# First gate chunks of the sparse block moved ahead of the keys and values, and the first block's input squared by tokens

## What is computed

```python
# first block
x = x + 0.5 * swiglu_ffn(rmsnorm(x, ffn1_norm), w_gate, w_up, w_down)    # width 1024 -> 2816 -> 1024
x = x + hybrid_mixer(rmsnorm(x, mix_norm), ...)
x = x + 0.5 * swiglu_ffn(rmsnorm(x, ffn2_norm), ...)
x = rmsnorm(x, final_norm)
# second block: twice x = layer_norm(alpha * x + mixer(x)); the sparse mixer, 8 heads of 128:
q, ckv, kr, qi, ki, wi, gate = split(x @ w_in)       # queries; 128-wide latent; 32-wide rotary key; index parts; gate 1024
q = rope(q); ckv = rms_norm(ckv); kr = rope(kr); qi = rope(qi); ki = rope(ki)
isc = sum_h(relu(qi_h . ki) * wi_h)                  # causal; each token keeps its 64 best keys
k = concat(ckv @ w_uk, kr); v = ckv @ w_uv           # in effect
o = softmax(q k^T over the kept keys) v
y = (silu(gate) * o) @ w_out
```

## Time and profile before

| | |
|---|---|
| median of three runs | 749.05 us (747.11 to 749.78) |
| the profiled execution | 747.19 us |
| its span in the trace | 745.4 us |
| TensorE busy, mean granted clock | 722.1 us (97%), 0.987 of full |
| VectorE, ScalarE, GpSimd busy | 447.5, 351.7, 73.0 us |
| HBM read | 126.77 MB, 171 GB/s over the span |

### The profile page before, as it was taken

One profiled execution on the slowest core, in us unless ns is written; L12 is line 12 of the kernel. 1 busy time (PEld: TensorE's weight loads), 2 busy tenths in 40 slices (PEclk: granted clock), 3 DMA queues, 4 the chain that ended last, 5 costly groups with the idle time before them and its releaser, 6 DMA issues.

```text
span 745.4 us, 11354 instructions
## 1 busy us (share of the span) xinstructions
PE 722.1 (97%) x4596; PEld 650.0 (87%) x4596; DVE 447.5 (60%) x707; ACT 351.7 (47%) x457; POOL 73.0 (10%) x43
## 2 busy tenths in 40 slices
PE   7999999999999999999999999999999999987985
PEld 6999999988887889999999888889998988766874
DVE  5875656655476446656566655485543657893655
ACT  5643334535377546534434444466335444564351
POOL 4000000000001320000000000000017260420002
PEclk8999999999999999999999999999999999999997
DMA  8986455545355344645545574265545133631001
GB/s 246 351 351 262 169 176 190 198 170 197 142 189 207 113 174 153 240 173 187 203 169 172 180 270 173 110 229 195 197 170 193 58 113 113 226 113 56 1 1 57
DMA packets 20535, 128.37 MB, mean 172 GB/s; under 512 B 2416, under 2 KB 3312, under 8 KB 6160
## 3 DMA queue, kind: packets, MB, share of 16 engines
q1 hardware_dynamic: 20448, 127.70, 48.0%
q0 software_dynamic: 48, 0.13, 0.1%
HBM read 126.77 MB, written 1.05 MB: 171 GB/s over the span
## 4 chain that ended last, share of the span: by engine, by line
PE 93%; DVE 2%; ACT 2%; DMA 1%; POOL 1%; issue 1%; SPq 0%; DVEq 0%; POOLq 0%; ACTq 0%
PE ps L368 29%; PE ps L370 28%; PE ps L369 28%; PE ps L565 1%; DMA work<-in_xt 1%; PE ps L379 1%; PE ps L622 1%; PE ps L621 1%; PE ps L903 1%; PE ps L620 1%; DVE wlo L1364 1%; PE ps L736 1%; ACT whi L978 1%; PE ps L892 0%; PE ps L611 0%
## 5 line engine op out<-in xcount | busy, mean ns | idle before, releaser
L368 PE MATMUL ps<-xth,whi 128*128 128x256 f32 x832 | 237.3, 285 | 4.4 <-DVE wlo L1501 4.4
L369 PE MATMUL ps<-xtl,whi 128*128 128x256 f32 x832 | 236.6, 284 | 0.0
L370 PE MATMUL ps<-xth,wlo 128*128 128x256 f32 x832 | 236.6, 284 | 0.0
L978 ACT ACTIVATE whi<-raw 128x2048 fp32r<-128x2048 f32 x78 | 148.6, 1909 | 100.3 <-PE ps L370 97.6
L1364 DVE TENSOR_TENSOR wlo<-raw,whi 128x2048 fp32r<-128x2048 f32 x68 | 156.7, 2314 | 64.3 <-ACT whi L978 64.2
L368 PEld LDWEIGHTS ps<-xth,whi 128*128 128x128 f32 x832 | 161.0, 194 | 5.2 <-DVE xtl L1377 5.1
L369 PEld LDWEIGHTS ps<-xtl,whi 128*128 128x128 f32 x832 | 161.0, 194 | 0.1
L370 PEld LDWEIGHTS ps<-xth,wlo 128*128 128x128 f32 x832 | 160.9, 193 | 0.0
L368 PE MATMUL ps<-whi,xth 128*128 128x512 f32 (+1 forms) x304 | 122.8, 404 | 3.2 <-DVE xtl L1493 2.0
L370 PE MATMUL ps<-whi,xtl 128*128 128x512 f32 (+1 forms) x304 | 117.9, 388 | 0.0
L369 PE MATMUL ps<-wlo,xth 128*128 128x512 f32 (+1 forms) x304 | 117.5, 387 | 0.0
(11 more groups left out here) (209 smaller groups left out, 681.0 us busy)
## 6 DMA issues: line engine op xcount, KB each, us to landing
raw<-in_gu SPq DMA_DIRECT2D x41, 1024.0 KB, 4.8
raw<-in_dn SPq DMA_DIRECT2D x22, 1024.0 KB, 4.7
raw<-in_win SPq DMA_DIRECT2D x8, 1024.0 KB, 4.8
raw<-in_fqk SPq DMA_DIRECT2D x8, 1024.0 KB, 5.0
raw<-in_wout SPq DMA_DIRECT2D x4, 1024.0 KB, 4.9
raw<-in_fg SPq DMA_DIRECT2D x4, 1024.0 KB, 5.0
raw<-in_fv SPq DMA_DIRECT2D x4, 1024.0 KB, 4.7
raw<-in_fo SPq DMA_DIRECT2D x4, 1024.0 KB, 4.7
```

The costliest lines, as they stand in the source:

```text
L368: pe.matmul(o, xh, wh, start=start, stop=False)
L369: pe.matmul(o, xh, wl, start=False, stop=False)
L370: return pe.matmul(o, xl, wh, start=False, stop=stop)
L978: act.activation(whi[:, c % RING, 0:n], raw[:, c % RING, 0:n], ACT.Copy).then_inc(hi_ready, 1)
```

## The change

In the first block: `sm` and the first piece of chunk 1 are issued by ScalarE; `X` is loaded in two halves right behind chunk 3, ahead of chunk 4; GpSimd's squares go, and `norm(0)` squares X on ScalarE (two passes), with the reciprocal and two diagonals on VectorE; the row is formed by TensorE in the middle of chunk 3, copied by ScalarE between the conversions of chunks 4 and 5, and VectorE scales chunk 0 behind the splits of chunks 4 and 5. In the sparse block: both gate chunks go into banks 2 and 3 around `turn_queries(1)`, ahead of the keys; heads 4 to 7 of the keys wait for the Silus (`gate_ready`); scores 0 and 1 come ahead of the values, which use banks 2 and 3 twice; ScalarE applies Silu and loads the Exp table ahead of the key copies, and copies the values between the first exponentials; the copy of bank 3 stands ahead of exps(4); four chunk conversions and four splits of the output chunks have other places.

```diff
@@ SP: loads @@
-            sp.dma_start(sm[:, :], a["sm"]).then_inc(sm_landed, 16)
...
-                for c in range(2):
+                for c in range(2 if i else 1):
                     sp.dma_start(raw[:, c, cols], a["gu0"][c][:, cols])...
...
             chunk(3, a["gu0"][3])
+            for t in range(NT):
+                sp.dma_start(X[:, t, :], a["x"][:, t, :]).then_inc(x_landed[t], 16)
             gate_up(0, (1, 3))
-            sp.dma_start(X[:, :, :], a["x"]).then_inc(x_landed, 16)
@@ TensorE, first block @@
-            def squares_to_row(bank):
...
             def rstd_to_row(i, bank, diagonal):
-                pe.wait_ge(diag_ready, 2 * i)
+                pe.wait_ge(eye_landed, 16)
+                pe.wait_ge(diag_ready, 2 * i + 2)
...
-                    for k, u in steps:
+                    for n_step, (k, u) in enumerate(steps):
+                        if f == 0 and static and j == 0 and i == 3 and n_step == KD:
+                            rstd_to_row(0, DOWN, ffn_diag)
...
                     first_pair()
-                    squares_to_row(DOWN)
@@ TensorE, sparse block @@
             turn_queries(0)
-
             pe.wait_ge(relu_ready, 2 * HI)
+            by_tokens(C_DG, 0, HALF, BANK, [2, 3], True, False)
+            turn_queries(1)
+            by_tokens(C_DG + 1, HALF, HALF, BANK, [2, 3], False, True)
+
             for h in range(H3):
+                if h == 4:
+                    pe.wait_ge(gate_ready, 6)
                 m = pe.matmul(ps[0:NOPE, h // 2, ...], uk[:, h, :], kvt, start=True, stop=True)
...
-            turn_queries(1)
-            for nb in range(2):
+            def expand_values(nb):
                 for t in range(NT):
-                    pe.wait_ge(k3_ready, 2 * nb + t + 1)
-                    pe.matmul(ps[:, 2 * nb + t, :], kvt[...], uv[...], start=True, stop=True).then_inc(v_psum, 1)
+                    if nb:
+                        pe.wait_ge(v3_ready, t + 1)
+                    pe.matmul(ps[:, 2 + t, :], kvt[...], uv[...], start=True, stop=True).then_inc(v_psum, 1)
...
-            pe.wait_ge(q3_ready, 2)
-            by_tokens(C_DG, 0, HALF, BANK, [4, 5], True, False)
             scores3(0)
             scores3(1)
-            by_tokens(C_DG + 1, HALF, HALF, BANK, [4, 5], False, True)
+            expand_values(0)
+            expand_values(1)
             pe.wait_ge(v3_ready, 4)
@@ ScalarE, first block @@
                 if f == 0:
-                    act.wait_ge(row_psum, 1)
-                    act.activation(ffn_row, ps[:, DOWN, 0:S], ACT.Sqrt, bias=eps_rms, scale=1.0 / D).then_inc(row_rms, 1)
+                    norm(0)
                     hi(C_GU[f] + RING)
                     load_table(ACT.Silu)
+                    row(f, DOWN, ffn_row)
                     hi(C_GU[f] + 1 + RING)
...
+            act.dma_start(sm[:, :], a["sm"]).then_inc(sm_landed, 16)
+            act.dma_start(raw[:, 1, 0:S], a["gu0"][1][:, 0:S]).then_inc(part_landed[1], 16)
             act.wait_ge(zeros_ready, 2)
@@ ScalarE, sparse block @@
             queries_out(1)
             turned_out(0)
+            hi(C_DQ + 3 + RING)
+            turned_out(1)
+            hi(C_DG + RING)
+            act.wait_ge(chunk_used, C_DG + 2)
+            for t in range(NT):
+                act.activation(gate3[:, t, 0:BANK], ps[:, 2 + t, :], ACT.Silu).then_inc(gate_ready, 1)
+            load_table(ACT.Exp)
             for p in range(4):
                 act.wait_ge(k_psum, p + 1)
                 act.activation(k3t[...], ps[0:NOPE, p, :], ACT.Copy).then_inc(k3_ready, 1)
-            turned_out(1)
...
-            hi(C_DQ + 3 + RING)
-            hi(C_DG + RING)
+            exps(2, 0)
+            values_expanded(0)
+            exps(2, 1)
+            values_expanded(1)
             hi(C_DG + 1 + RING)
-            for t in range(NT):
-                act.activation(gate3[:, t, 0:BANK], ps[:, 4 + t, :], ACT.Silu).then_inc(gate_ready, 1)
-            load_table(ACT.Exp)
-
-            for h in range(H3):
-                exps(2, h)
+            for h in range(2, H3):
                 if h == 4:
                     act.wait_ge(gate_psum, 1)
                     act.activation(gate3[:, 0, BANK:D], ps[:, 3, :], ACT.Copy).then_inc(gate_raw, 1)
+                exps(2, h)
                 if h == H3 - 2:
                     attn_hi(6, [4], 0)
+                    hi(C_DG + 2 + RING)
...
-            hi(C_DG + 2 + RING)
             hi(C_DG + 3 + RING)
@@ GpSimd @@
-            for i in range(4):
...
-                    pool.tensor_tensor(x_sq_sum, x_sq_sum, x_sq, ALU.add).then_inc(x_sq_summed, 1)
@@ VectorE @@
                 if f == 0:
-                    dve.wait_ge(row_rms, 1)
-                    dve.reciprocal(ffn_row, ffn_row).then_inc(row_ready, 1)
-                    dve.wait_ge(row_ready, 1)
-                    gate_and_up(0, 0)
+                    norm(0)
+                    dve.wait_ge(eye_landed, 16)
+                    diagonal(0, ffn_diag)
                 lo(C_GU[f] + RING)
                 lo(C_GU[f] + 1 + RING)
                 dve.wait_ge(row_ready, f + 1)
                 for i in range(4):
-                    if i or f:
-                        gate_and_up(0, i)
+                    gate_and_up(0, i)
...
             for h in range(H3):
-                if h in (2, 4):
+                if h in (3, 5):
                     lo(C_DO + h // 2 - 1)
...
+            lo(C_DO + 2)
             dve.wait_ge(gate_ready, 8)
             for g in (4, 5):
                 gated(2, g, gate3, pv_psum[2])
             probs_out(2, H3 - 1, 4)
             for g in (6, 7):
                 gated(2, g, gate3, pv_psum[2])
-            lo(C_DO + 2)
+            attn_lo(8, [6, 7], 4)
             lo(C_DO + 3)
-            attn_lo(8, [6, 7], 4)
```

More of the change, by code:

```diff
@@ L229, in build @@
         raw_landed = [sem(f"raw_landed{i}") for i in range(RING)]
-        x_landed, gains_landed, eye_landed = sem("x_landed"), sem("gains_landed"), sem("eye_landed")
+        x_landed, gains_landed, eye_landed = [sem(f"x_landed{t}") for t in range(NT)], sem("gains_landed"), sem("eye_landed")
         zeros_ready = sem("zeros_ready")
-        x_sq_ready, x_sq_summed, row_rms = sem("x_sq_ready"), sem("x_sq_summed"), sem("row_rms")
         sm_landed, xt_landed = sem("sm_landed"), [sem(f"xt_landed{i}") for i in range(len(PIECES))]
@@ L418, in by_tokens, with rstd_to_row @@
                 m.then_inc(chunk_used, 1)
-            def squares_to_row(bank):
+            def rstd_to_row(i, bank, diagonal):
                 pe.wait_ge(eye_landed, 16)
[L423 to L428, removed]
-                pe.wait_ge(diag_ready, 2 * i)
+                pe.wait_ge(diag_ready, 2 * i + 2)
                 for t in range(NT):
@@ L887, in _ @@
                     m.then_inc(k_psum, 1)
-            turn_queries(1)
-            for nb in range(2):
+            def expand_values(nb):
                 for t in range(NT):
-                    pe.wait_ge(k3_ready, 2 * nb + t + 1)
-                    pe.matmul(ps[:, 2 * nb + t, :], kvt[:, t * P:(t + 1) * P], uv[:, nb * BANK:(nb + 1) * BANK], start=True, stop=True).then_inc(v_psum, 1)
+                    if nb:
+                        pe.wait_ge(v3_ready, t + 1)
+                    pe.matmul(ps[:, 2 + t, :], kvt[:, t * P:(t + 1) * P], uv[:, nb * BANK:(nb + 1) * BANK], start=True, stop=True).then_inc(v_psum, 1)
             def scores3(h):
@@ L984, in norm @@
             def norm(r):
-                act.wait_ge(resid_done, 4 * r)
+                if r:
+                    act.wait_ge(resid_done, 4 * r)
+                else:
+                    act.wait_ge(chunk_used, 1)
                 for t in range(NT):
+                    if r == 0:
+                        act.wait_ge(x_landed[t], 16)
                     act.activation(XN[:, t, :], X[:, t, :], ACT.Square, accum_out=ss[:, t:t + 1]).then_inc(sumsq_ready, 1)
-                act.wait_ge(sumsq_ready, 2 * r)
+                act.wait_ge(sumsq_ready, 2 * r + 2)
                 act.activation(rms, ss, ACT.Sqrt, bias=eps_rms, scale=1.0 / D).then_inc(rms_ready, 1)
@@ L1090, in _ @@
             norm(1)
-            act.wait_ge(rstd_ready, 1)
+            act.wait_ge(rstd_ready, 2)
             for nb in range(3):
@@ L1141, in _ @@
             norm(3)
-            act.wait_ge(rstd_ready, 3)
+            act.wait_ge(rstd_ready, 4)
             for nb in range(2):
@@ L1249, in _, with values_expanded @@
                 act.activation(k3t[0:NOPE, 2 * p:2 * p + 2, :].rearrange("p h s -> p (h s)"), ps[0:NOPE, p, :], ACT.Copy).then_inc(k3_ready, 1)
-            turned_out(1)
-            act.wait_ge(isc_done, 2 * HI)
-            for nb in range(2):
+            def values_expanded(nb):
+                if nb == 0:
+                    act.wait_ge(isc_done, 2 * HI)
                 for t in range(NT):
                     act.wait_ge(v_psum, 2 * nb + t + 1)
```

(28 more changed lines are left out.)

8 lines of the change are left out of this document (2 added, 6 removed).

## The result

The changed kernel took 735.89 us in the median of four executions (735.19 to 737.6); the kernel before, beside it, 748.08 us (745.56 to 749.78, four). The ratio is 0.9849 with a 95% interval of 0.9826 to 0.9873, which is 11.3 us less; the two medians lie 12.2 us apart. The profiled execution took 737.6 us, its span is 735.8 us.

What follows compares the result with a forecast made beforehand. TensorE was taken as the bound (93% of the chain). Sparse block: 12.6 us removed, 2.6 added, net 10.0, taken as 9.8; first block 1.1 lost; 749.05 - 8.7 = 740.3 us, range 737.0 to 744.5.

Steps and rivals of the forecast that it cites:

- The added waits: Sparse block, new TensorE idle: 1.3 us before the first scores, 1.0 in the values, 0.3 at the last low parts.
- it now stands in front: Sparse block: bank 3's copy moves ahead of head 4's exponentials on ScalarE, so the 1.09 us gate-share wait goes.
- the two terms named for it: First block, third input piece: 0.6 us from earlier issue of loads, 1.3 us from cheaper VectorE low parts without GpSimd.
- it can't be shorter: First block: TensorE's new idle before chunk 4 is at least 3.0 us, a 5.8 us path less half a chunk, 2.8.
- other path: First block: chunk 4's landing, conversion, table, row, chunk 5 and scaling decide instead; 8.8 us from 26.8, start at 35.6.
- against the median, 749.05 - 8.7: Last step of the sum: the 8.7 us won, taken from the three runs' median 749.05, gives 740.3 us.
- with 3.0 us it more likely falls, 1.7 us: First block: TensorE's clock more likely falls at the new 3.0 us idle before chunk 4, costing 1.7 us.
- Rival (a): First block also wins: no clock drop at either gap, chunk 4 starts at 35.6; 11 us won, 738.0; chance 0.16.
- (b): ScalarE holds the sparse block up: new waits 2.3 + 2.0 us and one clock fall; 744.0 us; chance 0.13.
- (c): X delays the first block: chunk 4 lands at 29.0, clock falls at both gaps; 4.4 us lost, 743.6; chance 0.13.
- (d): Sparse block's head loop becomes bound by VectorE and ScalarE; slower, 751.5 us at 1.4 us per head; chance 0.03.
- (e): Edits miss the path: last wait is transposes, not splits; 4.07 us move to value copies; 4 won, 745.0; chance 0.08.

Runs made afterwards that it cites:

- experiment 6: Changed kernel with VectorE's splits of output chunks 0 to 3 back at their old places: 740.01 us, ratio 0.9911.
- experiment 8: Changed kernel with the copy of bank 3 behind head 4's exponentials again: 737.61 us, ratio 0.9869.
- experiment 3: Changed kernel with VectorE scaling chunk 0 ahead of the split of chunk 5 again: 734.18 us, ratio 0.9829.
- experiment 4: Changed kernel with the small constants and the first piece of chunk 1 issued by SP again: 738.64 us, ratio 0.9892.
- experiments 9 and 10: Idle TensorE matmuls: ten before chunk 4 on the changed kernel, 735.53 us; eight before the third input piece, with early scaling and shared key copies, 732.24 us.
- experiment 2: The first block's edits alone on the kernel before: 746.92 us, ratio 1.001.
- 11: The changed kernel timed a third time, unaltered, beside the kernel before: 736.33 us, ratio 0.9856.

## Why the prediction was off

**The sparse block: the waits right, the half clock a little too dear.** Forecast 9.8 us, measured 10.2 in the profiles, with these edits alone too. Removed were 2.00, 4.07, 1.09 and 2.03 us of waiting; experiment 6 gives the last of them back with the half clock behind it, 3.7 us. The added waits were forecast at 1.3, 1.0 and 0.3 us and are 1.21, 0.69 and nothing: 1.9 instead of 2.6. The two half-clock stretches were priced at 1.7 us each and cost 3.0 together. The 1.09 us is gone as the sum had it, but not by "it now stands in front": experiment 8 shows the copy in time either way.

**The first block: mechanism right, one step half a microsecond too long.** The pair of chunks ended at 21.6 us, forecast 21.5. The third piece's wait was forecast at 2.1 us and is 2.02, though 3.44 less the two terms named for it (0.6 and 1.3) is 1.5: the piece came 2.25 us earlier, but TensorE was also done with the second piece 0.83 us earlier, which the prediction did not say. The wait before chunk 4 was forecast at 3.0 us, and "it can't be shorter". It is 2.48 in the four profiles where TensorE's row is what ScalarE waits for: from the end of the row's products to chunk 4 it took 5.3 us, not 5.8. In the three others (2.63, 2.85 and 2.97 us) ScalarE copies the row right behind its table load, so the forecast's "other path" decides, and chunk 4 starts at 34.5 to 35.0, forecast 35.6. In the result's profile it starts at 36.01, forecast 36.2. The sum, 1.1 us lost, became 0.64 lost between the two profiles, and 1.001 (0.9997 to 1.0023) by timing.

**What failed: two steps on the way from the profile to the median.** Against the profiled execution the forecast said 747.19 - 8.7 = 738.5 us, and the profiled execution after took 737.6. The first failing step is "against the median, 749.05 - 8.7". The three runs shown were draws from a spread of over 4 us, and so was the 1.9 us by which the profiled one lay below their median: the kernel before had medians of 748.08, 746.38, 746.79 and 746.91 us in the four calls. I carried that chance offset over to the changed kernel. The second is "with 3.0 us it more likely falls, 1.7 us": I turned a chance into a fixed price. By their clock, four of fifteen executions had neither fall, among them two of the four of the result, and two falls are worth 2.8 us (735.1 against 737.9, the means of the table's first and last line), 1.4 each. Without the carried offset alone, the range would have begun at 735.1 and held 735.89. Rival (a), no fall at either wait, is what those two executions look like: 736.1 by its own terms without the offset, 735.19 and 735.39 measured.

**How much of the result is luck.** Over all calls the medians are 746.62 us (41 executions) and 737.43 (15): 9.2 us less, against 8.7 forecast. The result's own pair lies 12.2 us apart because three of its four executions of the kernel before lie above 747 us and two of its four of the changed kernel had no fall. So the edits are worth nearer to 9 us than to 12.

**The rivals.** (b), ScalarE holding the block up: its two waits are shorter than forecast. (c), X delaying the front: no, chunk 4 had landed by 25.95 us, not 29.0, and experiment 3 starts it without a wait with X where it is. (d), the head loop bound by VectorE: no idle time above 0.3 us in it. (e): experiment 6 shows that the splits were the wait.

**Open.** What the two loads on ScalarE's queue are worth in the total (experiment 4), and whether idle matmuls in a wait keep the clock up (experiments 9 and 10). Why a wait of 2.97 us in experiment 2 brought no fall while 2.48 us did in the profiles of the result and of experiments 4, 8 and 11: no run varied the wait's place in time alone.

## What to carry to other kernels

An edit that moves work off a full engine's critical list is priced by that engine's idle rows plus the half-clock stretches behind them; here that sum was right within half a microsecond, with 1.5 us for a stretch of 3.4. When a value is made later on purpose, follow who uses it next on every queue: the scaling behind one split cost what faster loads had won, and putting it back gave about 3 us (734.18 against the 737.43 of all fifteen, from different calls). Compare whole distributions by granted clock before carrying an offset between profile and median. The fastest version by its median (experiment 7, 732.1 us) is the changed kernel with the scaling ahead of the second split and the key copies shared.

## What the hardware showed beyond that

In the profiles here ahead of TensorE's last product its clock falls for 3.4 us or, once, 6.8 us at a time, and not behind every wait of the same length. Of the seven profiles with a wait of 2.5 to 3.0 us before chunk 4, six had a fall there and one, the longest with 2.97 us, had none. The wait for the rotated queries was 2.00 us before and in experiment 2: the clock fell in experiment 2 (661.7 to 665.1 us) and not in the kernel before. The wait before the last sums was 2.03 or 2.04 us in three profiles: the clock fell before and in experiment 6, and not in experiment 2. So a wait of 2 to 3 us is to be priced as a chance. A pair of VectorE's low parts, each with two operands in SBUF, slowed from 0.88 us to 2.17 and 2.69 while GpSimd multiplied and added operands of its own; the Trainium skill (GPSIMD Engine Reference, Key points) says that the two engines share their SBUF interfaces and get into each other's way when a VectorE instruction has two SBUF inputs, and the 2.17 against 0.88 us here agree.
